# Splitting the first weight unit in four blocks, taken in turn with the transpositions of x, and moving the SBUF buffers to multiples of 128 bytes

## What is computed

```python
xn = rms_norm(x, norm1_g)
proj = jnp.einsum('btd,dc->btc', xn, w_in)          # 1024 x 7168 weights, f32
b_a, c_a, h_a, glu_a, glu_b, g_in = jnp.split(proj, SPLITS, axis=-1)
y_a = (b_a * dwconv3(c_a * h_a)) @ w_out_a
y_b = silu(layer_norm(dwconv31(glu_a * sigmoid(glu_b)) + b)) @ w_out_b + b_out_b
x = x + (sigmoid(gA) * y_a + sigmoid(gB) * y_b) @ w_o
x = x + hier_moe(rms_norm(x, norm2_g))               # top 2 of 8 experts in the top group of 4
y = rms_norm(x, final_norm_g)
```

## Time and profile before

| | us |
|---|---|
| median of 3 runs | 850.46 |
| lowest, highest | 848.34, 850.73 |
| profiled execution | 847.72 |
| its span | 845.2 |

### The profile page before, as it was taken

How to read it: one execution, slowest core, us unless ns; L and a number is a source line. 1 busy time by engine, 2 the same in 40 slices (tenths; PEclk the granted TensorE clock), 3 DMA queues, 4 the chain that set the end, 5 groups by cost and what they waited for, 6 DMA issues and landing times.

```text
span 845.2 us, 21580 instructions
## 1 busy us (share of the span) xinstructions
PE 777.2 (92%) x8655; PEld 593.2 (70%) x8656; DVE 427.1 (51%) x1142; ACT 323.2 (38%) x559; POOL 258.5 (31%) x129
## 2 busy tenths in 40 slices
PE   3999999999999999999999989999899879989964
PEld 3999999999999999874555555555555545555532
DVE  4046978899994334144444433445333324334424
ACT  5333666655335833152332322322323213322224
POOL 3845699978576778300000000000000000000000
PEclk9999999999999999989999999999999999999997
DMA  7734343424444845974799999999999999999993
GB/s 253 228 101 150 100 125 125 150 92 144 152 167 150 299 140 214 329 320 147 307 415 419 421 421 421 419 420 421 422 420 419 421 421 422 420 420 420 422 420 153
DMA packets 53171, 249.98 MB, mean 296 GB/s; under 512 B 6599, under 2 KB 6599, under 8 KB 28561
## 3 DMA queue, kind: packets, MB, share of 16 engines
q1 hardware_dynamic: 49760, 246.95, 74.0%
q10 hardware_dynamic: 3377, 2.57, 1.3%
HBM read 246.76 MB, written 2.75 MB: 295 GB/s over the span
## 4 chain that ended last, share of the span: by engine, by line
PE 61%; DMA 21%; DVE 11%; ACT 3%; issue 2%; SPq 1%; POOL 1%; ACTq 0%; DVEq 0%
PE bank L1402 25%; DMA piece<-in_exp_w_up 20%; PE bank L1571 12%; DVE bank L1053 7%; PE bank L1600 7%; PE bank L1522 4%; PE bank L1559 4%; PE bank L1400 4%; PE bank L1587 1%; DVE sq L1115 1%; DMA raw<-in_w_in 1%; PE bank L1529 1%; SPq L548 1%; PE bank L1469 1%; PE bank L1463 1%
## 5 line engine op out<-in xcount | busy, mean ns | idle before, releaser
L602 POOL TENSOR_TENSOR w_lo<-raw,w_hi 128x2048 fp32r<-128x2048 f32 x40 | 184.9, 4624 | 76.5 <-ACT w_hi L721 76.4
L1571 PE MATMUL bank<-piece,xe 128*32 128x256 f32 x2816 | 168.7, 391 | 32.4 <-DMA piece<-in_exp_w_up 26.4
L1571 PEld LDWEIGHTS bank<-piece,xe 128*32 128x32 f32 x2816 | 97.2, 112 | 98.2 <-issue 48.0
L1402 PE MATMUL bank<-x_hi,w_hi 128*128 128x384 f32 x448 | 152.6, 341 | 1.2 <-POOL w_lo L602 1.1
L1402 PE MATMUL bank<-x_hi,w_lo 128*128 128x384 f32 x448 | 151.0, 337 | 0.0
L1402 PE MATMUL bank<-x_lo,w_hi 128*128 128x384 f32 x448 | 150.4, 336 | 0.0
L1053 DVE SCALAR_TENSOR_TENSOR bank<-ub,vec,bank 128x256 f32<-128x256 f32 (+1 forms) x416 | 137.1, 414 | 0.0
L721 ACT ACTIVATE w_hi<-raw 128x2048 fp32r<-128x2048 f32 x40 | 76.5, 1916 | 84.1 <-PE bank L1402 72.5
L1284 DVE SCALAR_TENSOR_TENSOR silu_and_hid<-bank,small,silu_and_hid 64x256 f32<-64x256 f32 x44 | 21.5, 489 | 170.3 <-ACT silu_and_hid L902 170.3
L1600 PE MATMUL bank<-piece,hidT 128*32 128x256 f32 x1408 | 94.2, 384 | 5.4
L1402 PEld LDWEIGHTS bank<-x_hi,w_hi 128*128 128x128 f32 x448 | 83.9, 187 | 2.3 <-POOL w_lo L602 1.3
(11 more groups left out here) (231 smaller groups left out, 983.7 us busy)
## 6 DMA issues: line engine op xcount, KB each, us to landing
piece<-in_exp_w_down SPq DMA_DIRECT2D x64, 1024.0 KB, 26.7
piece<-in_exp_w_gate SPq DMA_DIRECT2D x64, 1024.0 KB, 25.9
piece<-in_exp_w_up SPq DMA_DIRECT2D x64, 1024.0 KB, 27.0
raw<-in_w_in SPq DMA_DIRECT2D x28, 1024.0 KB, 5.2
raw<-in_w_out_a SPq DMA_DIRECT2D x4, 1024.0 KB, 5.1
raw<-in_w_out_b SPq DMA_DIRECT2D x4, 1024.0 KB, 5.3
raw<-in_w_o SPq DMA_DIRECT2D x4, 1024.0 KB, 5.0
out<-n_out SPq DMA_DIRECT2D x3, 512.0 KB, 3.3
```

Source lines behind the costliest of these rows:

```text
L602: pool.tensor_tensor(w_lo[u % NW][:, :, :], raw[u % NW][:, :, :], w_hi[u % NW][:, :, :].bitcast(F32), ALU.subtract).then_inc(lo_ready, 1)
L1402: ins = pe.matmul(b, wp[:, k % UK, cols], xp[:, k, :], start=start, stop=stop)
L1571: last = pe.matmul(GU[q * T:(q + 1) * T, :], xe[:, k, :], wide(pairs[q // 2], k)[:, q % 2 * QE:(q % 2 + 1) * QE], start=(k == 0), stop=(k ...
```

## The change

It does three things.

1. Unit 0 is handled by block. ACT writes w_hi of unit 0 in four instructions of 128 x 512, each ahead of x_hi of the same block; the first three end in a new semaphore `first_hi`, the last in `hi_ready`. Unit 1's w_hi moves from after x_hi 7 to between x_hi 3 and x_hi 4. POOL forms w_lo of unit 0 in four instructions (`first_lo`, `lo_ready`).
2. PE turns blocks 0, 1 and 2, and then for k = 0 to 3 issues eight products of block k (four groups with x_hi, four with x_lo) and turns block k + 3; then it turns block 7 and issues the 16 products with w_lo. The chunk loop skips unit 0. The 48 products are the same, in another order, with waits by block.
3. `small` shrinks from 48 to 32 columns, and `norm2_by_row`, `mark`, `zero`, `own_slot`, `slot_coef` and the second column set of the last sums move to a tile `few` behind the arena, which now starts at a multiple of 128 bytes.

```diff
@@ -163,12 +163,15 @@
         tmp = sb("tmp", [P, HALF // P, N])
         ident = sb("ident", [P, P])
         iota = sb("iota", [P, T])
-        small = sb("small", [P, 48])
-        norm2_by_row = sb("norm2_by_row", [P, KB])
-        same_at = nc.sbuf_base - 4 * (2 * KB * N + 4 * N + P + T + 48 + KB)
+        small = sb("small", [P, 32])
+        same_at = nc.sbuf_base - 4 * (2 * KB * N + 4 * N + P + T + 32)
         tmp_at = same_at + 2 * ACTS
         halves_at = nc.sbuf_base
+        assert halves_at % 128 == 0
         halves = sb("halves", [P, HALVES * 2048])
+        few = sb("few", [P, 24])
+        norm2_by_row, mark, zero = few[:, 0:KB], few[:, 8:14], few[0:1, 14:18]
+        own_slot, slot_coef, second_sums = few[:, 18:19], few[:, 19:20], few[:, 20:20 + NT]
 
         def at(name, shape, dt, offset):
             return nc.alloc_sbuf_tensor_at(name, shape, dt, offset=offset)
@@ -261,10 +264,6 @@
         lane = late("lane", [P, 1])
         rbias = late("rbias", [P, R])[:, :]
         down_rank = late("down_rank", [P, NE])[:, :]
-        mark = small[:, 36:36 + 6]
-        zero = small[0:1, 31:35]
-        own_slot = small[:, 45:46]
-        slot_coef = small[:, 46:47]
 
         ua_k = ua[:, :].rearrange("p (k n) -> p k n", k=KB)
         ub_k = ub[:, :].rearrange("p (k n) -> p k n", k=KB)
@@ -303,6 +302,8 @@
         rstd_ready = sem("rstd_ready")
         g_in = sem("g_in")
         unit_in = [sem(f"unit_in{i}") for i in range(NW)]
+        first_hi = sem("first_hi")
+        first_lo = sem("first_lo")
         hi_ready = sem("hi_ready")
         lo_ready = sem("lo_ready")
         half_done = sem("half_done")
@@ -602,7 +603,13 @@
                 pool.tensor_tensor(w_lo[u % NW][:, :, :], raw[u % NW][:, :, :], w_hi[u % NW][:, :, :].bitcast(F32),
                                    ALU.subtract).then_inc(lo_ready, 1)
 
-            low_part(0)
+            for k in range(UK):
+                if k < UK - 1:
+                    pool.wait_ge(first_hi, k + 1)
+                else:
+                    pool.wait_ge(hi_ready, 1)
+                pool.tensor_tensor(w_lo[0][:, k, :], raw[0][:, k, :], w_hi[0][:, k, :].bitcast(F32), ALU.subtract)\
+                    .then_inc(first_lo if k < UK - 1 else lo_ready, 1)
             low_part(1)
             for q, (s, half) in enumerate(CHUNKS):
                 if 2 * q + 2 < UNITS:
@@ -720,15 +727,20 @@
                     wait_unit_used(act, u - NW)
                 act.activation(w_hi[u % NW][:, :, :], raw[u % NW][:, :, :], ACT.Copy).then_inc(hi_ready, 1)
 
-            high_part(0)
-            act.wait_ge(dve_aux, 1)
+            act.wait_ge(unit_in[0], 16)
             for k in range(KB):
+                if k < UK:
+                    act.activation(w_hi[0][:, k, :], raw[0][:, k, :], ACT.Copy)\
+                       .then_inc(first_hi if k < UK - 1 else hi_ready, 1)
+                if k == 0:
+                    act.wait_ge(dve_aux, 1)
+                if k == UK:
+                    high_part(1)
 
                 a = aux("xT", k)
                 act.wait_ge(aux_done, a + 1)
                 act.activation(x_hi[:, k, :], bank[AUX_BANK[a]][:, 0:N], ACT.Copy, scale=vec[:, k, V_N1:V_N1 + 1])\
                    .then_inc(x_hi_ready, 1)
-            high_part(1)
             act.wait_ge(unit_in[1], 16)
             act.dma_start(stage[0:NS * HA, 1, :], cache_a.rearrange("l s h d -> (l s h) d")).then_inc(cache_in, 16)
             act.dma_start(cvb[0:NS // 2 * HB, :, :].rearrange("p k n -> p (k n)")[:, 0:2 * D].rearrange(
...
@@ -1369,12 +1381,48 @@
             for m in range(KB):
                 last = pe.transpose(b[:, m * NV:(m + 1) * NV], stage[0:NV, 0, m * P:(m + 1) * P], ident[0:NV, 0:NV])
             end_aux(last)
-            for k in range(KB):
+            def turn_x(k):
+
                 b = start_aux(aux("xT", k))
                 for i in range(NT):
                     pe.wait_ge(normed, i + 1)
                     last = pe.transpose(b[:, i * P:(i + 1) * P], n_tok[:, i, k * P:(k + 1) * P], ident[:, :])
                 end_aux(last)
+
+            def first_products(k):
+
+                if k < UK - 1:
+                    pe.wait_ge(first_hi, k + 1)
+                else:
+                    pe.wait_ge(hi_ready, 1)
+                pe.wait_ge(x_hi_ready, k + 1)
+                for j in range(HALF // P):
+                    pe.matmul(bank[j][:, 0:N], w_hi[0][:, k, j * P:(j + 1) * P], x_hi[:, k, :], start=(k == 0), stop=False)
+                wait_aux_read(pe, aux("xT", k))
+                for j in range(HALF // P):
+                    pe.matmul(bank[j][:, 0:N], w_hi[0][:, k, j * P:(j + 1) * P], x_lo[:, k, :], start=False, stop=False)
+
+            def first_low_products(k):
+
+                if k < UK - 1:
+                    pe.wait_ge(first_lo, k + 1)
+                else:
+                    pe.wait_ge(lo_ready, 1)
+                for j in range(HALF // P):
+                    last = pe.matmul(bank[j][:, 0:N], w_lo[0][:, k, j * P:(j + 1) * P], x_hi[:, k, :], start=False, stop=False)
+                return last
+
+            turn_x(0)
+            turn_x(1)
+            turn_x(2)
+            for k in range(UK):
+                first_products(k)
+                turn_x(k + 3)
+            turn_x(KB - 1)
+            for k in range(UK):
+                last = first_low_products(k)
+            last.then_inc(half_done, 1)
+
             def cached_rows():
 
                 pe.wait_ge(cache_in, 32)
@@ -1406,6 +1454,8 @@
                 groups = [i for i, x in enumerate(GROUPS) if x[2] == q]
                 for h in range(2):
                     u = 2 * q + h
+                    if u == 0:
+                        continue
                     pe.wait_ge(lo_ready, u + 1)
                     ready = {"Wa": (in_lo_ready, UK * (h + 1)), "Wb": (in_lo_ready, KB + UK * (h + 1)),
                              "Wo": (merged_lo_ready, UK * (h + 1))}.get(s)
```

More of the change, by code:

```diff
@@ L922, in last_square @@
                     act.wait_ge(weighted, 2 * n + 1)
-                at_col = (16, 42)[h] + i
+                sums = (small[:, 16:16 + NT], second_sums)[h]
                 act.activation(squares[:, :], total(i, h)[:, :], ACT.Square, scale=1.0 / ROOT_D,
-                               accum_out=small[:, at_col:at_col + 1]).then_inc(ssq_ready, 1)
+                               accum_out=sums[:, i:i + 1]).then_inc(ssq_ready, 1)
             def root(n):
@@ L1319, in mean_square @@
                 dve.wait_ge(ssq_ready, 2 * NT + 2 * n + 2)
-                dve.scalar_tensor_tensor(small[:, 20 + i:21 + i], small[:, 16 + i:17 + i], 1e-6, small[:, 42 + i:43 + i],
+                dve.scalar_tensor_tensor(small[:, 20 + i:21 + i], small[:, 16 + i:17 + i], 1e-6, second_sums[:, i:i + 1],
                                          ALU.add, ALU.add).then_inc(root_in, 1)
```

## The result

| | us |
|---|---|
| median of 6 runs | 844.82 (843.38 to 845.30) |
| median of 6 runs of the kernel before, beside them | 850.87 (848.34 to 852.11) |
| ratio, 95% interval | 0.9926 (0.9911 to 0.9940) |
| span of the profiled execution | 841.6 (before 845.2) |

The change makes the kernel 6.0 us faster, 5.1 to 7.6 by the interval. The forecast was 848.8 with a range of 845.4 to 851.2, and within 0.3% as the likeliest class: wrong in both.

The account below looks back on a forecast made before the run. TensorE was taken to bound the mixer and DMA loads the experts, so a 1.6 us earlier unit 1 passes through: span 845.2 less 1.6, plus 2.5 around it and 2.7 to the median, 848.8 us; alignment 0; range 845.4 to 851.2.

Parts of the forecast that it names:

- the alignment, taken as 0: Arena tiles moving 96 bytes down to a multiple of 128: taken as 0 for both loads and engines.
- the pair of x_hi and x_lo: Products moving x_hi (aligned) took 341 ns, x_lo (96 past) 336: no cost of the old offset seen.
- The bounds from the earlier trace: Expert loads over 382 us, from window rates of 420 to 424 GB/s: a gain of 2.7 or loss of 0.9.
- Alignment speeds the loads: Rival, chance 0.15: aligned destinations speed the loads by 2.7 us, to 846.1; by the skill page 844.4.
- the split as forecast: Unit 0 split and interleaved: it ends at 25.7 instead of 27.30 us, gain 1.6 us.
- three signs: Forecast wrong if PE waits for w_lo at unit 1, loads reach 424 GB/s, or products are 0.35 us apart past 20.
- the clock's rise near 17: PE's clock at the start: 1.2 GHz until about 17.0 us, 2.4 GHz after; the sum used 17.05.
- POOL's margin of 1.1 us at unit 1: Unit 1's w_lo ready on POOL about 24.6 us, wanted by PE at 25.7; the thinnest margin.
- The early clock: Rival, chance 0.08: PE's clock rises before 17.05; about 847.6 us at a rise near 14.6.
- The gain that doesn't arrive: Rival, chance 0.17: unit 1's w_lo late on POOL, or another queue takes over, eating 1.6 us: 850.4.
- the clock staying low into the stream: Rival, chance 0.06: low clock into the mixed stream; loses from a rise about 20.2, costs 2.4 at 25: 852.9.
- The rule on transpositions and the clock: Skill page at PE's start: transpositions don't count as clock activity, so the half-transposition stream would rise later.

Follow-up runs that it names:

- f_arena_256: f_after with the arena alone 128 bytes further, on a multiple of 256, the x_hi tile staying 128 past one: 840.56 us.
- f_after: The whole change, with TensorE's loop bounds loaded five at once and their limits asserted behind: 843.97 us, 0.9940 of f_before.
- f_warm_before: f_before with 45 extra transpositions of the identity before TensorE's wait for the vector loads: 849.73 us.
- f_256_warm60: f_after with x_hi's tile and the arena on multiples of 256, plus 60 extra identity transpositions at the start: 835.39 us, 0.9833 of the kernel before.
- e_arena_64: The whole change with loop bounds loaded one by one (847.58 us), the arena moved to 64 bytes past a multiple of 128: 848.73 us.
- f_split: f_before with only the split and interleaved first unit, the arena still 96 past a multiple of 128: 847.23 us, 0.9974 of f_before.
- f_warm_split: f_after with 45 extra transpositions of the identity before TensorE's wait for the vector loads: 842.82 us.
- c_before_v: The kernel before, with TensorE loading its item-loop bounds one by one with asserted limits instead of five at once: 853.58 us, 1.0055 of before.
- f_before: The kernel before, with bounds still loaded five at once and only their limits asserted behind: 849.83 us, 1.0002 of before.

## Why the prediction was wrong

**The term that failed is the alignment, taken as 0.** Alone it is worth 3.7 us of 6. Two steps failed in it.

- *For the engines, the pair of x_hi and x_lo.* The step read the earlier trace rows by each moved tile's own start: x_hi, aligned, took 341 ns and x_lo, 96 past, 336, so the old offset seemed to cost nothing. But the weights lie in the arena with x_lo. The rows compare products whose two tiles start at different places (x_hi) with products whose tiles start at the same place (x_lo), and the first kind is the slower. The same rows after the change (difference 0) and in f_arena_256 (difference 128) bear this out; they are shown behind this list. With equal starts the two come to within 3 ns, with a difference of 128 they are 12 apart. So the pair pointed at the cost and was read the wrong way round. It doesn't give the size by itself: the durations are 5 ns apart, the mean distance between starts changed by 1.5. The kernel before had a comparison for that too: the window 302 to 322, where nearly all operands lie in the arena, holds 117 products in 20 us (173.3 ns by their starts), and the mixed stream 517 in 90 (174.8). Neither was looked at. Size of this term: taken as 0, measured 1.9 to 2.0 us over the products of the mixer.
- *For the loads, the 0.* The bounds from the earlier trace rows were -2.7 and +0.9. 420.5 to 421.8 GB/s is 1.5 us by the estimate above and lies within them; the value taken was wrong, the bounds were right. The forecast gave "Alignment speeds the loads" 0.15 and priced it at 846.1. The time of the change, 844.8, is near its page estimate of 844.4, but by luck: of the layout's 3.5 us (2.0 and 1.5) more than half come from PE's spacing, for which there was no rival.

The rows named in the first point, after, then f_arena_256:

```profile
L1450 PE MATMUL bank<-x_hi,w_hi 128*128 128x384 f32 x432 | 145.4, 337 | 0.3 <-DVE ua L1084 0.2
...
L1450 PE MATMUL bank<-x_lo,w_hi 128*128 128x384 f32 x432 | 144.4, 334 | 0.0
...
L1452 PE MATMUL bank<-x_hi,w_hi 128*128 128x384 f32 x432 | 148.8, 344 | 0.1
...
L1452 PE MATMUL bank<-x_lo,w_hi 128*128 128x384 f32 x432 | 143.5, 332 | 0.0
```

The terms add up to 5.1 us with the split as forecast (1.6, 2.0 and 1.5); measured are 6.0, with an interval that begins at 5.1. None of the three signs that the prediction named for its being wrong came: PE did not wait for w_lo at unit 1, the loads stayed under 424 GB/s, and no product past 20 us was 0.35 us from the next. They guarded the split and a large load effect, not the spacing.

The Trainium skill, "DMA: Bandwidth & Descriptors", "How a descriptor splits into AXI transactions", has the place right: only a start on a multiple of 256 makes the step to 427 GB/s, 1.35% above 421.8, where an estimate by its beats, 260 against 256, would be 1.6%. The same estimate has the smaller step too large: 263 against 260 beats would be 1.1%, measured 0.3% (420.5 and 421.8). And it speaks of bytes fetched; here the source did not move and the destination did, and the rate changed.

**The split was right in mechanism and near in size.** PE's stream from 12.1 us without a stop, the clock's rise near 17, POOL's margin of 1.1 us at unit 1, the quarters' durations, the loads of the cache under cover: all seen. A product at the low clock was booked at 0.35 us and takes 0.32. Unit 1 was forecast at 25.7 and starts at 25.56 (25.37 and 25.40 in later traces). By the medians the split gives 1.8 to 2.6, where 1.6 was forecast.

**The rivals.** The early clock did not come (the high level begins at 17.16, and at 16.50 in f_after). The gain that doesn't arrive, and the clock staying low into the stream, neither: from the clock's rise on, products stay 0.175 or 0.173 apart. The low clock under the products did come in f_warm_before, where it cost 1.6 us at unit 1. The rule on transpositions and the clock from the Trainium skill ("TensorE: Matmul & The Clock Gate", "Part 4: PE-mode transpose") was set aside by the earlier trace rows, and f_256_warm60 shows the same: PE did nothing but transpositions until 13.47, and its first products run at the high level.

**The range** ended at 845.4, 0.6 us above the time. The forecast less the loads' whole bound of 2.7 is 846.1, so the range did hold all that was asked of the loads; what it had no room for is the spacing's 2.0 on top.

## What to carry to other kernels

Price a moved buffer by the distance between starts, counted in equal windows, and by comparing stretches whose operands lie in different tiles. When two kinds of products are compared, write down where both operands lie, not the moved one alone. Start tiles that one stream of matmuls reads together at the same place modulo 256, and the targets of large loads on a multiple of 256. When work moves ahead of the rise of TensorE's clock, count it at the low rate, and see whether idle engine time before it can be filled right up to it: with a pause of 1.7 to 2.0 us behind the filling the low level came back.

## What the runs showed of the hardware

- f32r products of 384 columns start 173.3 ns apart when x_hi's tile and the arena begin at the same place modulo 256, 174.4 at a difference of 32 or 64, 174.8 at 96 and 175.6 at 128. In the mixer's last stage (512 columns) 226.7, 233.3 (difference 32), 228.9 (64), 231.1 (96) and 233.3 ns (128). At the low clock they start 320 ns apart at differences of 0, 64, 96 and 128 alike (after, e_arena_64, f_split, f_arena_256). Why the difference counts is open.
- 8 KB rows into the arena run at 420.4 to 420.6 GB/s from a start of 224 modulo 256, at 421.8 to 422.0 from 128, 160 and 192, and at 427.5 to 427.6 from 0 (window 500 to 800 us), with the loads themselves unchanged.
- TensorE's rate doubled during a stretch of transpositions alone (213 to 109 ns from start to start at 6.0 us in f_warm_split). There TensorE then stood still for 1.7 us (9.4 to 11.1), and the granted clock was low from 12.86 to 16.27; in f_warm_before, with a pause of 2.0 us, from 12.44 to 22.68. In f_256_warm60, with no idle time over 0.2 us between 2.6 and 23.6 us, it rose at 6.93 and stayed high there.
- One register load after another is dear at a loop's head: five single loads with asserted limits, in place of one load of five values, made TensorE stand 3.8 us a round (c_before_v) instead of 0.9 (before) or 1.2 (f_before, with the limits asserted behind the one load).
